# Where a kernel's weights and activations lie in the scratchpad: two weight rings 64 bytes higher, one layer's output 112 bytes higher

## The reference, cut to what matters

```
(silu(h @ w_gate) * (h @ w_up)) @ w_down        # widths 1024 -> 2816 -> 1024
```

## Time and profile before

| | |
|---|---|
| median of three runs | 2483.31 us (2483.14 to 2483.47) |
| the profiled execution's own time | 2483.6 us |
| its span, first to last instruction | 2481.8 us |
| granted clock of TensorE, mean | 1.00 |
| busy: PE, PEld, DVE, ACT, POOL | 2461.1, 2070.7, 1415.2, 1045.7, 986.5 us |
| mean HBM traffic | 91 GB/s |

### The profile page before, as it was taken

The page is one execution under the profiler, slowest core; times in us unless marked ns, Lnnn a source line. Parts: engine busy times, 40 slices in busy tenths (PEclk is TensorE's granted clock), DMA queues, the critical chain, the costliest instruction groups (busy, mean ns, idle before and its releaser), DMA issues.

```text
span 2481.8 us, 37092 instructions
## 1 busy us (share of the span) xinstructions
PE 2461.1 (99%) x13516; PEld 2070.7 (83%) x13516; DVE 1415.2 (57%) x1904; ACT 1045.7 (42%) x1566; POOL 986.5 (40%) x729
## 2 busy tenths in 40 slices
PE   9999999999999999999999999999999999999999
PEld 9999999957777789988776788888887678888887
DVE  7988114376446679931696656653355845665213
ACT  5556224375334455542574322232244842322222
POOL 3001553303224430055352655554453055555443
PEclk9999999999999999999999999999999999999999
DMA  4333333202112233333321323222232223222322
GB/s 163 109 103 94 109 102 102 80 1 60 60 60 90 97 102 110 106 116 103 102 94 43 102 93 101 93 97 98 93 128 82 64 85 102 94 100 94 110 93 85
DMA packets 72764, 230.97 MB, mean 93 GB/s; under 512 B 9361, under 2 KB 9745, under 8 KB 72658
## 3 DMA queue, kind: packets, MB, share of 16 engines
q1 hardware_dynamic: 64704, 216.27, 26.8%
q10 hardware_dynamic: 7954, 13.26, 1.7%
HBM read 220.58 MB, written 5.24 MB: 91 GB/s over the span
## 4 chain that ended last, share of the span: by engine, by line
PE 94%; DVE 4%; ACT 1%; issue 1%; DMA 0%; POOL 0%; SPq 0%; DVEq 0%; ACTq 0%
PE PS L306 24%; PE PS L308 24%; PE PS L307 23%; PE PS L895 5%; PE PS L897 4%; PE PS L896 4%; PE PS L2297 1%; DVE ast__155 L3569 0%; PE PS L1939 0%; PE PS L2323 0%; PE PS L1920 0%; PE PS L2958 0%; PE PS L2309 0%; PE PS L2969 0%; PE PS L3542 0%
## 5 line engine op out<-in xcount | busy, mean ns | idle before, releaser
L300 POOL TENSOR_TENSOR wlo<-wraw,whi 128x512 fp32r<-128x512 f32 (+2 forms) x351 | 462.3, 1317 | 1425.0 <-ACT whi L292 1424.9
L306 PE MATMUL PS<-xh,whi 128*128 128x512 f32 (+1 forms) x1672 | 621.1, 371 | 1.6 <-POOL wlo L301 0.8
L308 PE MATMUL PS<-xh,wlo 128*128 128x512 f32 (+1 forms) x1672 | 614.1, 367 | 0.0
L307 PE MATMUL PS<-xl,whi 128*128 128x512 f32 (+1 forms) x1672 | 613.8, 367 | 0.0
L292 ACT ACTIVATE whi<-wraw 128x1024 fp32r<-128x1024 f32 (+2 forms) x351 | 351.2, 1002 | 592.5 <-PE PS L308 578.9
L301 POOL TENSOR_TENSOR wlo<-wraw,whi 128x512 fp32r<-128x512 f32 (+2 forms) x351 | 524.7, 1495 | 0.0
L306 PEld LDWEIGHTS PS<-xh,whi 128*128 128x128 f32 x1672 | 313.4, 187 | 58.0 <-issue 2.2
L308 PEld LDWEIGHTS PS<-xh,wlo 128*128 128x128 f32 x1672 | 313.4, 187 | 52.6
L307 PEld LDWEIGHTS PS<-xl,whi 128*128 128x128 f32 x1672 | 313.5, 187 | 52.3 <-issue 1.4
L306 PE MATMUL PS<-hid2h,whi 128*128 128x512 f32 x560 | 218.4, 390 | 0.0
L307 PE MATMUL PS<-hid2l,whi 128*128 128x512 f32 x560 | 217.9, 389 | 0.0
(11 more groups left out here) (558 smaller groups left out, 5033.9 us busy)
## 6 DMA issues: line engine op xcount, KB each, us to landing
wraw<-w_up_dram SPq DMA_DIRECT2D x96, 512.0 KB, 3.2
wraw<-w_dn_dram SPq DMA_DIRECT2D x48, 512.0 KB, 3.2
wraw<-w_f2gu_dram SPq DMA_DIRECT2D x44, 512.0 KB, 3.3
wraw<-w_f1gu_dram SPq DMA_DIRECT2D x41, 512.0 KB, 3.2
wraw<-w_hyin_dram SPq DMA_DIRECT2D x24, 512.0 KB, 3.2
wraw<-w_win_dram SPq DMA_DIRECT2D x18, 512.0 KB, 3.2
wraw<-w_gate_dram SPq DMA_DIRECT2D x16, 512.0 KB, 3.2
wraw<-w_pg_dram SPq DMA_DIRECT2D x16, 512.0 KB, 3.2
```

Of the source, the lines that this page charges most:

```text
L300: pool.tensor_tensor(wlo[:, s, 0:half], wraw[:, s, 0:half], whi[:, s, 0:half].bitcast(F32), ALU.subtract)
L306: pe.matmul(out_, whi[:, s, a:b], xhi, start=start, stop=False, skip_group_check=True)
L307: pe.matmul(out_, whi[:, s, a:b], xlo, start=False, stop=False, skip_group_check=True)
L308: return pe.matmul(out_, wlo[:, s, a:b], xhi, start=False, stop=stop, skip_group_check=True)
```

## The change

Offsets change and, with them, two waits. `whi` and `wlo` begin 64 bytes further up, `h` and everything behind it 128. `yh`, `yl` and four tiles that share their place or lie behind them move another 112 bytes within the area, to multiples of 128. `oph` and `opl` now begin where the rings begin, in both gated layers: for `f1gu` that is 64 bytes further up than before, for `f2gu` the same place. As ring slots and operand slots coincide, `f2gu` asks for one used chunk less before its operands 0 and 3, and 4 and 5, like `f1gu`.

```diff
-        o_raw, o_hi, o_lo = 0, 16384, 32768
-        o_h = 49152
+        o_raw, o_hi, o_lo = 0, 16448, 32832
+        o_h = 49280
...
-        yh = at("yh", B + 49296, [P, 8, T], F32R)
-        yl = at("yl", B + 65680, [P, 8, T], F32R)
-        xc = at("xc", B + 82064, [P, 4, T])
+        yh = at("yh", B + 49408, [P, 8, T], F32R)
+        yl = at("yl", B + 65792, [P, 8, T], F32R)
+        xc = at("xc", B + 82176, [P, 4, T])
...
-        mnum = at("mnum", B + 82064, [P, 2, T])
-        mden = at("mden", B + 86160, [P, T])
-        macc = [at("macc0", B + 95568, [P, T]), at("macc1", B + 88208, [P, T])]
+        mnum = at("mnum", B + 82176, [P, 2, T])
+        mden = at("mden", B + 86272, [P, T])
+        macc = [at("macc0", B + 95568, [P, T]), at("macc1", B + 88320, [P, T])]
...
-            o_op = 0 if H == 2 else 64
-            oph = at(name + "oph", o_hi + o_op, [P, 7, 512], F32R)
-            opl = at(name + "opl", o_lo + o_op, [P, 7, 512], F32R)
+            oph = at(name + "oph", o_hi, [P, 8, 512], F32R)
+            opl = at(name + "opl", o_lo, [P, 8, 512], F32R)
...
-                    free_after(p, 4, 2 if H == 2 else 3)
+                    free_after(p, 4, 2)
...
-                    free_after(p, 6, 3 if H == 2 else 4)
+                    free_after(p, 6, 3)
```

## The result

| | before | after |
|---|---|---|
| median | 2483.22 us (2482.82 to 2483.47, 4 runs) | 2499.47 us (2496.48 to 2502.08, 4 runs) |
| profiled execution, its span | 2483.6, 2481.8 us | 2496.91, 2495.1 us |
| PE busy, PEld busy | 2461.1, 2070.7 us | 2475.1, 2072.8 us |

The ratio is 1.0065, 95% interval 1.0048 to 1.0083: slower, where 2481.7 us (2475.5 to 2487) was forecast. The four times after are two pairs, 2496.5 and 2496.9, 2502.0 and 2502.1. The kernel before has such a pair too: in later series 2482.5 to 2483.9 in 14 of 55 runs, and 2488.0 to 2489.1 in the rest.

What follows compares the result with a forecast made beforehand. TensorE's time from one matmul start to the next was taken as the bound. Output move -1.3, second gated layer's opening -0.3, the rest 0: -1.6 us takes 2483.6 to 2482.0; the timed median, 0.3 lower, gives 2481.7, range 2475.5 to 2487.

Steps and rivals of the forecast that it cites:

- So 512-wide stays at 226.7 and 264-wide at 121.9, a cost of 0: Moving rings and activations leaves matmul start-to-start times, in ns, unchanged for 512-wide tiles and the first gated layer: 0 us.
- what changes is the distance [...] modulo 128: Weights being loaded against row being streamed: 0 before, 64 after for 512-wide tiles; second gated layer's products already at 64.
- Slower: Rival, chance 0.13: constant distance 64 costs 5616 512-wide matmuls at L306 to L308 6.6 ns each, 37 us, giving 2518.7.
- tile 1: Latent queries' projection, 512-wide rows at stride 2112 bytes: distance 64, 233 ns, the rows that disagreed with no cost.
- lines of 16 bytes: Rival unit by which an offset of 16 is already aligned; moving `yh` then gains nothing, 2483.0 us, chance 0.11.
- -1.3 forecast: Recurrent layer's output, `yh` and `yl` moved to multiples of 128: 192 matmuls gain 6.6 ns each, taken as 1.3 us.
- 33rd piece: `yh` and `yl` rows at offset 16 touch an extra 64-byte piece, 233.3 ns against 226.7 for 32 pieces.
- One formula fits all four: Matmul times before read as 64-byte pieces touched: 226.7 ns is 32, 113.4 is 16, 233.3 is 33, 264-wide slightly over.
- the 5.4 either way: 264-wide matmuls, 3624 together, 1.5 ns over their pieces: at most 5.4 us could go or be added, 0 taken.
- 0 was right: VectorE and ScalarE access to the moved rings: split of 1024 columns stays at 1225 ns, off the path, 0 us.
- The opening, -0.3 forecast: Second gated layer's start: fewer chunk waits let the seed and L895 follow earlier, 0.3 us gained, between 0 and 0.38.
- under 0.2: Sign in the profile after: the gap ahead of L895 in the second gated layer's opening falls below 0.2 us.

Runs made afterwards that it cites:

- D = 64: D is the rows' place minus the weights' place, in bytes; for most 512-wide matmuls the change moved it from 0 to 64, 2499.47 us.
- the bare ones: Whole computation left out, TensorE alone running matmuls at chosen places of rows and weights; 512 wide 226.7, 229.0, 232.4, 233.3 ns at distances 0, 64, 128, 192.
- -1.2 alone: Kernel before with only the recurrent output and its four neighbours moved 112 bytes up, rings left in place; 2481.95 us profiled, the others 2487.1 to 2487.8.
- one cut matmul: Kernel before plus the output's move, one product in the second gated layer's second block done as two 128-column matmuls; 2481.91 to 2482.62 us, ratio 0.9981.
- the kernel at D = 192: Changed kernel with everything behind the rings 128 bytes higher, so the rows' place minus the weights' is 192; 2530.0 us, ratio 1.0167 against the kernel before.

## Why the prediction was wrong

The step that failed is "So 512-wide stays at 226.7 and 264-wide at 121.9, a cost of 0", for the 512-wide. The value was taken from the earlier trace rows, on the ground that "what changes is the distance [...] modulo 128". Two things in that were untested. The period is 256: the products of the earlier trace rows stood at 448, that is 192, and not at 64. And 256 columns say nothing of 512: where the one is fastest (192) the other is slowest, and at 0 the reverse. Rows of 512 columns at 64 existed, in the earlier trace rows; they were set aside because their distance jumps from tile to tile, and because 128 came out no better than 64, which refuted the modulus and not the rows. What the runs showed in its place: at a constant D = 64 a 512-wide matmul takes 228.9 ns, 2.2 more, and most of the 6654 matmuls pay it.

The rival "Slower" had the mechanism, its place and its sign; its price of 6.6 ns, from tile 1 of the earlier trace rows, was three times too high: 13.5 us on the 6654 matmuls of the first three groups are 2.0 ns each, the bare ones 2.3. 6.6 is what 192 costs. Tiles 0, 1 and 2 stand at 0, 64 and 128, and 227, 233 and 235 from two or three steps read to 10 ns were too coarse to take a price from; the bare runs have 226.7, 229.0 and 232.4 in the same order. The trace before had longer rows of this kind, in the first block's mixer: 512 columns at a stride of 2112 bytes, 12 matmuls to a tile. Timeline of PE, before, the first rows of tiles 1 to 6:

```profile
381.79 0.40 PE L306 MATMUL PS<-xh,whi 128*128 128x512 f32 x1
...
384.56 0.40 PE L306 MATMUL PS<-xh,whi 128*128 128x512 f32 x1
...
387.35 0.39 PE L306 MATMUL PS<-xh,whi 128*128 128x512 f32 x1
...
390.15 0.39 PE L306 MATMUL PS<-xh,whi 128*128 128x512 f32 x1
...
392.89 0.40 PE L306 MATMUL PS<-xh,whi 128*128 128x512 f32 x1
...
395.65 0.40 PE L306 MATMUL PS<-xh,whi 128*128 128x512 f32 x1
```

Each difference over 12, the change of tile included: 230.8, 232.5, 233.3, 228.3 and 230.0 ns for tiles 1 to 5. Tile 4, 256 bytes from tile 0, is fast again and tile 5 is like tile 1: the period and a price of 2 to 3 ns stood there.

With nothing else at work the weights' place alone moves the time from 226.7 (0) to 233.3 ns (16, 32 or 48 further up). The Trainium skill's rule that loading weights takes no read bandwidth from the running matmul ("TensorE: Matmul & The Clock Gate", "Step-by-step: what each phase is for") doesn't agree with that: by it the place would not show. The Trainium skill's lines of 16 bytes ("SBUF — State Buffer", "Specifications (TRN2)") don't describe these rows either: rows and weights both at 16 take 231.1, both at 32 226.7.

`yh`: -1.3 forecast, -1.2 alone, -0.8 after the change, since it too then stands at 64. The size was right by luck and the reason wrong: no 33rd piece, but the pair of places. "One formula fits all four" was four numbers fitted by a rule that the bare runs refute (226.7 with both at 32).

The products of the second gated layer kept their 113.3 ns by luck too: they went from 192 to 64, which isn't the same distance as the prediction had it, and 64 happens to have that rhythm as well. The 264-wide: +0.8 us in all, inside the 5.4 either way. VectorE's split of 1024 columns has a median of 1226 ns in both layers after the change (1225 in the earlier trace rows): 0 was right. The opening, -0.3 forecast; timeline of ACT, after:

```profile
915.91 0.63 ACT L1004 ACTIVATE f2guoph<-wraw 128x512 fp32r<-128x512 f32 x1 [4.43 <-PE PS L308]
917.11 1.06 ACT L957 ACTIVATE hid2h<-f2gupr 128x1024 fp32r<-128x1024 f32 x1 [0.56 <-DVE f2gupr L1117]
```

and of PE:

```profile
918.37 0.28 PE L896 MATMUL PS<-f2gutops,f2guopl 128*128 128x256 f32 x1
918.59 0.36 PE L894 MATMUL PS<-f2gutops,f2guoph 128*128 128x256 f32 x1
```

VectorE's result is late next, as forecast, and the step ahead of L894 (L895 before) is 0.22 us where the earlier trace rows have 0.49: 0.27 us gained there, though not "under 0.2". The first block of products as a whole takes 10.30 us against 10.35, since a step near its end, at 924.21, takes 0.30 us where it took 0.12: nearly nothing of the 0.3 is left.

What stays open: which read waits for which, why the period is 256 bytes, why rows and weights both at 16 or 48 are slow while both at 32 are not, and what makes the entry differ between two executions of one kernel. The runs show only that the places of weights and rows and the width, with nothing else at work, decide which steady rhythms there are, and the entry which of them holds.

## What to carry to other kernels

Where TensorE never waits, the offsets of weights and moving rows are a tuning parameter of their own: measure the time from start to start at each distance for the very width that is used, bare and from several entries, before the layout is changed. Don't carry a value from one width to another, and try a period on rows that could refute it. When one kernel's times come in two groups, look for a stage whose steady rhythm is set by how it is entered; one cut matmul can fix it (here 0.1 us for the 5.5 of the executions that would have had the slower rhythm).

## What had not been expected of the hardware

At one distance (192) the same products run at 113.3 ns a matmul for 14 blocks on end (the kernel before) or at 117.8 (the kernel at D = 192), and a cut of one matmul turns the one into the other; 512 wide at 64 has 228.9 and 233.3. A distance that is best for 512 columns (0: 226.7) is the worst for 256 (120.0 against 113.3 at 192).
